# Linear attention: fine levels reduced to diagonal 32x32 blocks, with compact masked copies

## The chip, the cores and the metric

The kernel runs on one NeuronCore of a Trainium2 chip. The metric is the device time of one execution in microseconds, the median over several runs. A measurement of this kernel tells a change from no change at about 0.2%, which is about 4 us.

## The reference, cut to what matters

The program computes two transformer blocks over 512 tokens. The change lies in the gated linear attention of the first block: 4 heads, 64 key channels and 128 value channels each, run forward and backward, with a decay for each channel. Inside a chunk every pair of a query i and a key j has its own decay:

```python
rel = cum[:, :, :, None, :] - cum[:, :, None, :, :]
decay = jnp.exp(jnp.where(mask[:, :, None], rel, -jnp.inf))
attn = jnp.einsum('bhid,bhjd,bhijd->bhij', qc, kc, decay)
o = o_inter + jnp.einsum('bhij,bhje->bhie', attn, vc)
```

`o_inter` is the query, decayed, times the state that the earlier chunks left.

## The kernel before, in words

The kernel takes tiles of 128 tokens (4 of them, for 4 heads) and builds the 128 by 128 matrix of a tile and head, `attnT` (keys on partitions, queries in columns), level by level. `LEVELS` are the spans s = 64, 32, 16, 8, 4, 2, 1. At level s the pairs whose two tokens lie in neighbouring blocks of s inside one block of 2s are decayed through the boundary between the two blocks, so that the decay splits into a factor for the query and a factor for the key. Level 0 in the code (`li` = 0) is the diagonal, and `li` = 1 to 7 are the seven spans.

One level takes these steps, in this order:

- VectorE (`sums`, L1519 to L1532) writes four differences of running sums: two halves of `lk`, then two halves of `lq`, each of 128x512 elements.
- ScalarE (`level_decay`, L1410) takes the exponential of `lk`, then of `lq`, in place.
- GpSimd (`gla_gpsimd`, L1599) multiplies `lk` with the keys, and VectorE (L1549) multiplies `lq` with the queries.
- TensorE (`gla_level`, L1280) forms, for both heads of a pair, all tiles and both directions, the whole 128x128 products into four PSUM banks.
- The part of the level is copied out of PSUM into `attnT`: for `li` 1 and 2 by ScalarE in blocks (`blocks`, L1415), for `li` 0 and 3 to 7 by VectorE under a mask of 128 columns (`attention`, L1505), four instructions of 128x512 elements a level.

`lq` and `lk` have two buffers each (`lq_even`, `lq_odd`), so the steps of level `li` + 1 run while TensorE works on level `li`. VectorE does the copy of level `li` - 1 behind the sums of `li` + 1. GpSimd's and VectorE's programs are in a fixed order, written out by hand, and engines wait for each other by semaphores. A PSUM bank is taken by `claim`, which waits until the reader before has counted `bank_empty`.

Around this stage: level 0 is formed on TensorE (L1289) in the middle of four "spreads" (L1316, a transposition that spreads a norm factor over the columns, two heads ahead of level 0 and two behind it). Their results go through VectorE (L1246, L1239) and ScalarE (L1432) into `hh` and `hl`, which `mixed_values_chunk` (L1386) multiplies with a weight (L441). Its first chunk claims PSUM bank 1, which level 0 has used. After the last level TensorE adds the share of the states to the outputs (`from_states`, L1341), multiplies `attnT` with the values (`within`, L1347), sums squares (`output_sums`, L1357), and the output projection follows (L441).

On TensorE a float32 matmul is two records in the trace, so "x32" there stands for 16 matmuls of the program.

The constants of the first block lie in one tile, `csta`, which one transfer loads (L2892). Before, it holds eight masks of 128 columns.

## Time and profile before

| | |
|---|---|
| median of 3 runs | 2075.94 us (2074.49 to 2076.79) |
| the profiled execution | 2078.38 us, of which its span from the first to the last instruction is 2076.4 us |
| TensorE (PE) busy | 1976.8 us of the span, 9954 matmul records |
| VectorE (DVE) busy | 929.1 us |
| ScalarE (ACT) busy | 745.2 us |
| GpSimd (POOL) busy | 706.1 us |
| mean granted clock of TensorE | 0.969 of full speed |

Busy time is an average over stages with different limits. The stage that the change touches lies between about 341 and 443 us of the span; the rest of the program is untouched, save for the load of `csta` at 50 us. A profile's row tells its start, its length, the engine, the line of the kernel, what is written and read, how many equal ones are merged, and in brackets how long the engine sat idle before it and who ended that.

### The profile page before, as it was taken

The numbers are of one execution on the slowest core, as the hardware profiler recorded it, in microseconds if no ns is written. First come the engines' busy times: TensorE is split into PE (matmuls) and PEld (weight loads), VectorE is DVE, ScalarE is ACT, GpSimd is POOL, SyncE is SP. The second block draws the span as 40 slices with busy tenths as digits, with TensorE's granted clock in tenths as the row PEclk, the third lists the DMA queues.
The fourth block names the chain that finished last, engine by engine and source line by source line (L and its number), as shares of the span: only waits on it lengthen the run. The fifth ranks groups of instructions, "written<-read, shape, count | busy, mean of one in ns | idle before, by whom it ended". The sixth has DMA issues, their size and how long they took to land.

```text
span 2076.4 us, 25531 instructions
## 1 busy us (share of the span) xinstructions
PE 1976.8 (95%) x9954; PEld 1561.8 (75%) x9954; DVE 929.1 (45%) x1358; ACT 745.2 (36%) x1235; POOL 706.1 (34%) x296
## 2 busy tenths in 40 slices
PE   7999988799999999999999989889999999999998
PEld 5787857687888888788888867656876768888886
DVE  2642586844444420444443334676776522332102
ACT  4533364533322311432322134546255432323222
POOL 1421110423444444344444433220421343444442
PEclk9999998879999999999999999999999999999999
DMA  7751110013444442334445422200210222232231
GB/s 309 299 210 41 42 62 1 21 41 104 150 146 147 161 173 91 112 132 146 147 149 194 173 77 82 71 32 21 92 62 31 82 81 82 100 94 98 92 100 61
DMA packets 60125, 223.60 MB, mean 108 GB/s; under 512 B 6800, under 2 KB 7056, under 8 KB 58256
## 3 DMA queue, kind: packets, MB, share of 16 engines
q1 hardware_dynamic: 59472, 220.13, 30.7%
q10 hardware_dynamic: 576, 2.43, 0.3%
q8 instruction: 50, 0.82, 0.2%
q14 instruction: 27, 0.22, 0.0%
HBM read 220.43 MB, written 2.10 MB: 107 GB/s over the span
## 4 chain that ended last, share of the span: by engine, by line
PE 86%; DVE 7%; ACT 3%; issue 2%; DMA 1%; SPq 0%; POOL 0%; DVEq 0%; ACTq 0%
PE ps L441 75%; DVE neg_max L1197 1%; PE ps L587 1%; DMA mod_w<-mod_w 1%; PE ps L2231 1%; ACT w_hi L454 1%; PE ps L1052 1%; PE ps L2402 1%; PE ps L2423 0%; PE ps L1071 0%; PE ps L2253 0%; PE ps L974 0%; PE ps L2411 0%; DVE ps L693 0%; DMA raw<-stream 0%
## 5 line engine op out<-in xcount | busy, mean ns | idle before, releaser
L1820 POOL TENSOR_TENSOR w_lo<-raw,w_hi 128x1024 fp32r<-128x1024 f32 x276 | 668.1, 2421 | 1295.9 <-ACT w_hi L454 696.0
L441 PE MATMUL ps<-hh,w_hi 128*128 128x512 f32 (+1 forms) x1512 | 605.3, 400 | 21.2 <-DVE hl L679 8.8
L441 PE MATMUL ps<-hl,w_hi 128*128 128x512 f32 (+1 forms) x1512 | 595.9, 394 | 0.0
L441 PE MATMUL ps<-hh,w_lo 128*128 128x512 f32 (+1 forms) x1512 | 595.2, 394 | 0.0
L441 PEld LDWEIGHTS ps<-hh,w_hi 128*128 128x128 f32 (+1 forms) x1512 | 287.7, 190 | 94.7 <-issue 30.3
L441 PEld LDWEIGHTS ps<-hh,w_lo 128*128 128x128 f32 (+1 forms) x1512 | 287.5, 190 | 62.4
L441 PEld LDWEIGHTS ps<-hl,w_hi 128*128 128x128 f32 (+1 forms) x1512 | 288.0, 190 | 58.1
L1793 ACT ACTIVATE w_hi<-raw 128x1024 fp32r<-128x1024 f32 x126 | 133.8, 1062 | 478.0 <-PE ps L441 478.0
L507 DVE SCALAR_TENSOR_TENSOR mod_raw<-mod_raw,cond_ada 128x1024 f32<-128x1024 f32 x72 | 118.1, 1642 | 245.6 <-DMA mod_raw<-late 245.6
L441 PE MATMUL ps<-act_hi,w_hi 128*128 (+1 forms) x528 | 208.8, 396 | 0.0
L441 PE MATMUL ps<-act_lo,w_hi 128*128 (+1 forms) x528 | 208.8, 396 | 0.0
L441 PE MATMUL ps<-act_hi,w_lo 128*128 (+1 forms) x528 | 208.8, 396 | 0.0
L1853 DVE TENSOR_TENSOR act_lo<-prod,act_hi 128x512 fp32r<-128x512 f32 x66 | 157.6, 2388 | 57.5 <-ACT act_hi L1798 57.5
L1812 ACT ACTIVATE w_hi<-raw 128x1024 fp32r<-128x1024 f32 x60 | 63.6, 1061 | 266.2 <-PE ps L441 266.2
L454 ACT ACTIVATE w_hi<-raw 128x1024 fp32r<-128x1024 f32 x90 | 94.7, 1055 | 146.9 <-PE ps L441 144.5
L1850 DVE TENSOR_TENSOR prod<-silu,ps 128x512 f32<-128x512 f32 x66 | 45.4, 688 | 222.3 <-PE ps L441 208.9
L441 PEld LDWEIGHTS ps<-act_lo,w_hi 128*128 128x128 f32 x528 | 99.2, 188 | 24.0
L441 PEld LDWEIGHTS ps<-act_hi,w_lo 128*128 128x128 f32 x528 | 99.2, 188 | 24.0
L441 PEld LDWEIGHTS ps<-act_hi,w_hi 128*128 128x128 f32 x528 | 99.2, 188 | 23.9
L1677 DVE SCALAR_TENSOR_TENSOR xT<-ps,half_gate_f,xT 128x512 f32<-128x512 f32 x16 | 11.2, 749 | 137.7 <-PE ps L441 137.7
L1677 DVE SCALAR_TENSOR_TENSOR xT<-ps,mod,xT 128x512 f32<-128x512 f32 x24 | 17.5, 750 | 92.7 <-PE ps L441 92.6
L507 DVE SCALAR_TENSOR_TENSOR early_raw<-early_raw,cond 128x1024 f32<-128x1024 f32 x32 | 48.5, 1542 | 15.5 <-DMA early_raw<-early 9.5
(432 smaller groups left out, 2340.7 us busy)
## 6 DMA issues: line engine op xcount, KB each, us to landing
raw<-stream SPq DMA_DIRECT2D x284, 512.0 KB, 3.3
mod_raw<-late SPq DMA_DIRECT2D x72, 512.0 KB, 4.4
early_raw<-early SPq DMA_DIRECT2D x32, 512.0 KB, 6.4
mod_w<-mod_w SPq DMA_DIRECT2D x8, 1024.0 KB, 20.1
xT<-xT SPq DMA_DIRECT2D x2, 1024.0 KB, 6.3
xT<-xT ACTq DMA_DIRECT2D x2, 1024.0 KB, 6.3
out<-fin SPq DMA_DIRECT2D x8, 256.0 KB, 2.2
csta<-csta SPq DMA_DIRECT2D x1, 1344.0 KB, 5.7
```

The lines of the kernel that those rows point to most:

```text
L441: mm = pe.matmul(out, w, r, start=first and i == 0, stop=last and i == 2)
L454: act.activation(halves_of(g)[0][:, :], raw[slot_of[g] % RING][:, :], ACT.Copy).then_inc(S("w_hi_ready"), 1)
L507: dve.scalar_tensor_tensor(out=slot, in0=slot, scalar=1.0, in1=condition, op0=ALU.mult, op1=ALU.mult, accum_out=to)\
L587: mm = pe.matmul(ps[32 * q:32 * q + 32, ba, 0:tokens], c("one").broadcast_to([P, 32]), squares(key, k, tokens), start=(k < 4), stop=(k >= ...
L1052: mm = pe.matmul(flat[:, r * 1024 + a:r * 1024 + z], dq[rows, h, qt * P:(qt + 1) * P], dk[rows, h, a:z], start=True, stop=True)
L1197: dve.tensor_reduce(neg_max[u % 2][:, comp:comp + 1], flat[:, r * 1024:r * 1024 + NALL], AX, ALU.max, negate=True)\
L1677: dve.scalar_tensor_tensor(out=xT[:, m, :], in0=ps[:, b, :], scalar=gate(m), in1=xT[:, m, :], op0=ALU.mult, op1=ALU.add)\
L1793: act.activation(w_hi[g % SPLIT][:, :], raw[n % RING][:, :], ACT.Copy).then_inc(S("w_hi_ready"), 1)
L1812: act.activation(w_hi[g % SPLIT][:, :], raw[n % RING][:, :], ACT.Copy).then_inc(S("w_hi_ready"), 1)
L1820: pool.tensor_tensor(lo[:, :], raw[n % RING][:, :], hi[:, :].bitcast(F32), ALU.subtract)\
L1850: dve.tensor_tensor(prod[j][:, :], silu[j][:, :], ps[:, b + 1, :], ALU.mult).then_inc(bank_empty(b + 1), 1)
L1853: dve.tensor_tensor(act_lo[:, at], prod[j][:, :], act_hi[:, at].bitcast(F32), ALU.subtract).then_inc(S("act_ready"), 1)
```

## The change

- `li` 0 and 3 to 7 (the diagonal and the spans up to 16) form only the four diagonal blocks of 32x32 of each tile: 64 matmuls with 32 weight columns and 32 moving columns each, for 16 with 128 and 128. They write two PSUM banks, one for each head of a pair (`fine_bank`), 256 columns of each.
- VectorE's masked copy goes from those banks to a compact tile `diag` ([128, 4, 4, 32]), two instructions of 128x256 elements a level for four of 128x512. The masks have 32 columns.
- After the last level `diag` is put into the diagonal blocks of `attnT`: two copies on VectorE and two on ScalarE, 32 partitions and 512 elements each. `within` waits for all four (`diag_ready`).
- The last level (s = 1) has no `lk` of its own: its factor is 1, so TensorE reads the keys. Two of VectorE's sums, one of ScalarE's exponentials and one of GpSimd's products go away.
- The copies of `li` 1 and 2 on ScalarE no longer wait for the level before, since they write other blocks.
- `from_states(0)` moves from ahead of the last level to ahead of the last but one, and `from_states(1)` from behind the last level to ahead of it.
- `csta` shrinks from 2688 to 1856 columns.

```diff
-for _name, _w in (("rot", 128), ("cos", 512), ("sin", 512), ("carry", 512), ("levels", 128 * (1 + len(LEVELS)))):
+for _name, _w in (("rot", 128), ("cos", 512), ("sin", 512), ("carry", 512), ("fine", 32 * (1 + len(LEVELS) - COARSE))):
...
+    fine_bank = {0: 0, 3: 4, 4: 6, 5: 4, 6: 6, 7: 4}
+    def gla_level(pe, li):
...
+        if li in fine_bank:
+            for half in range(2):
+                claim(pe, fine_bank[li] + half, ("level", li, half))
+            for u in range(2 * NT):
+                for half in range(2):
+                    rows = slice(64 * half, 64 * half + 64)
+                    for o in range(0, P, 32):
+                        at = (u % 2) * N + (u // 2) * P + o
+                        mm = pe.matmul(ps[o:o + 32, fine_bank[li] + half, u * 32:u * 32 + 32], k[rows, at:at + 32], q[rows, at:at + 32],
+                                       start=True, stop=True)
+                    if u == 2 * NT - 1:
+                        mm.then_inc(bank_full(fine_bank[li] + half), 1)
+            return
...
         for li in range(1, len(LEVELS) + 1):
-            if li == len(LEVELS):
+            if li == len(LEVELS) - 1:
                 pe.wait_ge(S("qe_ready"), 2)
                 read(pe, ("u", len(directions) - 1, 4))
                 from_states(0)
+            if li == len(LEVELS):
+                from_states(1)
             pe.wait_ge(S("lq_ready"), li)
-            pe.wait_ge(S("lk_ready"), li)
+            if li < len(LEVELS):
+                pe.wait_ge(S("lk_ready"), li)
             gla_level(pe, li)
-        from_states(1)
-        for b in range(4):
-            read(pe, ("level", len(LEVELS), b))
+        pe.wait_ge(S("diag_ready"), 4)
         within(0)
...
+        for o in (0, 32):
+            act.activation(attnT[o:o + 32, :, :, o:o + 32], diag[o:o + 32, :, :, :], ACT.Copy).then_inc(S("diag_ready"), 1)
...
         def attention(li):
-            mask = ca("levels", li * P, (li + 1) * P).unsqueeze(1).unsqueeze(1).broadcast_to([P, 2, 2, P])
-            for b in range(4):
+            at = 32 * (li - COARSE if li else 0)
+            mask = ca("fine", at, at + 32).unsqueeze(1).unsqueeze(1).broadcast_to([P, NT, 2, 32])
+            for half in range(2):
...
-            mark("level_sums", dve.tensor_tensor(to_k[:, :, 0, :], mid_f, fw[:, :, 0, :], ALU.subtract))
-            mark("level_sums", dve.tensor_tensor(to_k[:, :, 1, :], mid_b, bw[:, :, 1, :], ALU.subtract))
+            if s > 1:
+                mark("level_sums", dve.tensor_tensor(to_k[:, :, 0, :], mid_f, fw[:, :, 0, :], ALU.subtract))
+                mark("level_sums", dve.tensor_tensor(to_k[:, :, 1, :], mid_b, bw[:, :, 1, :], ALU.subtract))
...
         attention(len(LEVELS))
+        for o in (64, 96):
+            dve.tensor_copy(attnT[o:o + 32, :, :, o:o + 32], diag[o:o + 32, :, :, :]).then_inc(S("diag_ready"), 1)
...
-        for li in range(1, len(LEVELS) + 1):
+        for li in range(1, len(LEVELS)):
             pool.wait_ge(S("lk_decay"), li)
             pool.tensor_tensor(lk[li % 2][:, :], lk[li % 2][:, :], k, ALU.mult).then_inc(S("lk_ready"), 1)
```

On TensorE, from level 5 (s = 4) to the products with the values, the program of before reads as follows (a matmul of the program is one here; L1289 is a level, L1341 the states' share, L1347 the product with the values):

```order
L1289 MATMUL ps<-lq_odd,lk_70 128x128 x16
L1289 MATMUL ps<-lq_even,lk_69 128x128 x16
L1341 MATMUL ps<-qe,states 128x128 x16
L1289 MATMUL ps<-lq_odd,lk_70 128x128 x16
L1341 MATMUL ps<-qe,states 128x128 x16
L1347 MATMUL ps<-attnT,vt 128x128 x12
```

and the changed one, where L1301 is a level, L1364 the states' share and L1370 the product with the values:

```order
L1301 MATMUL ps<-lq_odd,lk_70 32x32 x64
L1364 MATMUL ps<-qe,states 128x128 x16
L1301 MATMUL ps<-lq_even,lk_69 32x32 x64
L1364 MATMUL ps<-qe,states 128x128 x16
L1301 MATMUL ps<-lq_odd,gkx 32x32 x64
L1370 MATMUL ps<-attnT,vt 128x128 x12
```

Both shares of the states have moved one place up, and the last level now stands directly ahead of the products with the values.

On VectorE, from the product for level 6 (L1549) to the outputs (L1567), before:

```order
L1549 TENSOR_TENSOR lq_even<-lq_even,gqx 128x1024
L1529 TENSOR_TENSOR lk_70<-cumx 128x512
L1530 TENSOR_TENSOR lk_70<-cumx 128x512
L1531 TENSOR_TENSOR lq_odd<-cumx 128x512
L1532 TENSOR_TENSOR lq_odd<-cumx 128x512
L1516 COPY_PREDICATED attnT<-csta,ps 128x4x128 x4
L1549 TENSOR_TENSOR lq_odd<-lq_odd,gqx 128x1024
L1516 COPY_PREDICATED attnT<-csta,ps 128x4x128 x8
L1567 SCALAR_TENSOR_TENSOR og<-ps,vec,rT 128x512 x2
```

and of the change (L1583 is the product, L1549 the masked copy):

```order
L1583 TENSOR_TENSOR lq_even<-lq_even,gqx 128x1024
L1565 TENSOR_TENSOR lq_odd<-cumx 128x512
L1566 TENSOR_TENSOR lq_odd<-cumx 128x512
L1549 COPY_PREDICATED diag<-csta,ps 128x8x32 x2
L1583 TENSOR_TENSOR lq_odd<-lq_odd,gqx 128x1024
L1549 COPY_PREDICATED diag<-csta,ps 128x8x32 x4
L1600 COPY attnT<-diag 32x16x32 x2
L1605 SCALAR_TENSOR_TENSOR og<-ps,vec,rT 128x512 x2
```

The two sums for `lk` are gone, the masked copies are half as many and a quarter of the elements, and two copies into `attnT` stand behind the last one.

## Rows read from the trace of the kernel before

**Rows 1.** The page, part 1: busy time, share of the span, instructions of each engine.

```profile
PE 1976.8 (95%) x9954; PEld 1561.8 (75%) x9954; DVE 929.1 (45%) x1358; ACT 745.2 (36%) x1235; POOL 706.1 (34%) x296
```

**Rows 2.** The chain that ended last, around level 0: start us, us, what.

```profile
339.80 1.94 PE ps L1316 x8
341.74 4.89 PE ps L1289 x32
346.63 1.02 PE ps L1316 x8
347.65 4.72 issue
352.37 4.93 PE ps L441 x12
```

**Rows 3.** Timeline of VectorE between level 0 and the first chunk.

```profile
347.25 0.75 DVE L1246 SCALAR_TENSOR_TENSOR t<-od,gain_dn,ps 128x512 f32<-128x512 f32 x1 [4.12 <-PE ps L1316]
...
350.98 2.48 DVE L1514 TENSOR_TENSOR attnT<-ps,csta 128x512 f32<-128x512 f32 x4
```

**Rows 4.** Timeline of all engines but TensorE, levels 5 to 7.

```profile
408.32 1.22 DVE L1549 TENSOR_TENSOR lq_odd<-lq_odd,gqx 128x1024 f32<-128x1024 f32 x1
...
410.78 1.06 ACT L1413 ACTIVATE lk<-lk 128x1024 f32<-128x1024 f32 x1 [3.73 <-DVE lk L1530]
...
411.85 2.58 DVE L1516 COPY_PREDICATED attnT<-csta,ps 128x512 f32<-128x512 uint32 x4
411.92 2.37 POOL L1603 TENSOR_TENSOR lk<-lk,gkx 128x1024 f32<-128x1024 f32 x1 [3.62 <-ACT lk L1413]
411.98 1.06 ACT L1413 ACTIVATE lq_even<-lq_even 128x1024 f32<-128x1024 f32 x1
414.30 1.24 DVE L1549 TENSOR_TENSOR lq_even<-lq_even,gqx 128x1024 f32<-128x1024 f32 x1
...
420.29 1.24 DVE L1549 TENSOR_TENSOR lq_odd<-lq_odd,gqx 128x1024 f32<-128x1024 f32 x1
```

**Rows 5.** Timeline of TensorE: levels 2, 5 and 6, states' share, values.

```profile
388.81 2.82 PE L1289 MATMUL ps<-lq_even,lk 64*128 64x128 f32 x32 [0.48 <-DVE lq_even L1549]
...
409.59 3.79 PE L1289 MATMUL ps<-lq_odd,lk 64*128 64x128 f32 x32 [1.27 <-DVE lq_odd L1549]
415.59 5.13 PE L1289 MATMUL ps<-lq_even,lk 64*128 64x128 f32 x32 [2.21 <-DVE lq_even L1549]
422.92 3.79 PE L1341 MATMUL ps<-qe,states 64*128 64x128 f32 x32 [2.20 <-DVE attnT L1516]
...
431.73 2.94 PE L1347 MATMUL ps<-attnT,vt 128*128 128x128 f32 x24
```

**Rows 6.** Timelines of VectorE and GpSimd, level 3.

```profile
392.29 2.27 DVE L1549 TENSOR_TENSOR lq_odd<-lq_odd,gqx 128x1024 f32<-128x1024 f32 x1 [1.12 <-ACT lq_odd L1413]
...
391.13 2.35 POOL L1603 TENSOR_TENSOR lk<-lk,gkx 128x1024 f32<-128x1024 f32 x1 [4.44 <-ACT lk L1413]
```

**Rows 7.** Windows: stretch, length, busy by engine, granted clock (PEclk), DMA share, GB/s.

```profile
412.00:416.00 4.00, 1.79 (x11) 1.50 (x10) 4.00 (x6) 1.04 (x1) 2.28 (x1) 0.50 0.00 0
...
428.00:430.00 2.00, 2.00 (x32) 2.00 (x32) 1.52 (x3) 0.00 (x0) 0.00 (x0) 0.94 0.44 166
```

**Rows 8.** Timeline of TensorE: small or narrow matmuls elsewhere in the program.

```profile
1518.09 0.24 PE L2402 MATMUL ps<-step,table_part 128*32 128x128 bf16 x3
...
1518.39 0.22 PE L2402 MATMUL ps<-step,table_half 128*32 128x128 bf16 x1
...
357.23 1.31 PE L1329 MATMUL ps<-vt,kdT 128*64 128x128 f32 x20
```

**Rows 9.** Around the load of `csta`: the chain, a window, TensorE's wait.

```profile
51.42 8.58 DMA raw<-stream
...
60.00:70.00 10.00, 7.83 (x33) 4.52 (x32) 7.82 (x9) 8.01 (x15) 4.52 (x2) 0.83 1.01 399
...
65.01 0.92 PE L587 MATMUL ps<-sq_context,cst 128*32 128x256 f32 x4 [1.99 <-ACT sq_context L624]
```

More of the change, by code:

```diff
@@ L41 @@
 LEVELS = [64, 32, 16, 8, 4, 2, 1]
+COARSE = 2
 GRID_W = 64
@@ L232, in build @@
     lq = [sb("lq_even", [P, 2 * N]), lq_odd]
+    top[0] = region_dn
+    diag = sb("diag", [P, NT, HEADS, 32])
     top[0] = region
@@ L1418, in blocks @@
                 at_bank = full(act, ("level", li, b))
-                read(act, ("level", li - 1, b))
                 got = ps[:, at_bank, :].rearrange("p (t h i) -> p t h i", t=2, h=2)
@@ L1450, in gla_scalar @@
         split_slots(act, firsts["mix1"] + 1)
+        read(act, ("level", len(LEVELS), 0))
+        read(act, ("level", len(LEVELS), 1))
+        for o in (0, 32):
+            act.activation(attnT[o:o + 32, :, :, o:o + 32], diag[o:o + 32, :, :, :], ACT.Copy).then_inc(S("diag_ready"), 1)
         def output_high(h):
@@ L1522, in sums @@
             if li >= 3:
-                full(dve, ("level", li - 2, 3))
+                full(dve, level_done(li - 2))
             fw, bw = halves(cumx[:, 0, :], s), halves(cumx[:, 1, :], s)
@@ L1562, in gla_vector @@
         attention(len(LEVELS))
+        read(dve, ("level", len(LEVELS), 0))
+        read(dve, ("level", len(LEVELS), 1))
+        for o in (64, 96):
+            dve.tensor_copy(attnT[o:o + 32, :, :, o:o + 32], diag[o:o + 32, :, :, :]).then_inc(S("diag_ready"), 1)
         def gated_output(h):
@@ L2962, in constants @@
     put(first, CSTA, "carry", (t % P != 0)[None, :])
-    levels = [2.0 * np.eye(P)] + [(p[:, None] // (2 * s) == p // (2 * s)) & (p[:, None] // s != p // s) for s in LEVELS]
-    put(first, CSTA, "levels", np.concatenate(levels, axis=1))
+    here = p[:, None] % 32
+    there = np.arange(32)
+    fine = [2.0 * (here == there)] + [(here // (2 * s) == there // (2 * s)) & (here // s != there // s) for s in LEVELS[COARSE:]]
+    put(first, CSTA, "fine", np.concatenate(fine, axis=1))
     return stay, first
```

21 lines of the change are left out of this document (14 added, 7 removed).

## The prediction

> **What bounds the kernel now.** I read the page first. TensorE is busy for 95% of the span [rows 1], so what counts are the places where it waits or does little work for its time. Then I followed the chain of waits through the stage of the change, and read the timelines engine by engine, since the chain alone does not say who would be late next.
>
> Around level 0 the chain runs through TensorE itself. Two spreads are done, then the level's 32 records take 4.89 us, then come the other two spreads, and then TensorE stands still for 4.72 us until the first chunk of the projection [rows 2]. The timelines say what it stands for: the spread behind level 0 releases VectorE at 347.25, VectorE works through to 350.98, and there it copies level 0 out of four banks [rows 3]. The chunk claims bank 1, the second of the four. The copies start 0.6 us apart, so bank 1 is free near 352.3, and the chunk starts at 352.37. Level 0 and half of its copy are both on the path.
>
> From level 4 on the kernel runs in a cycle of 6.0 us: VectorE's product for `lq` starts at 408.32, 414.30 and 420.29 [rows 4]. Inside a cycle VectorE has no free time: product, four sums, four masked copies of 0.6 us. But a second chain has the same length. From the start of one product it is 2.46 us to ScalarE's exponential of `lk` (410.78), then GpSimd's product from 411.92 to 414.29. VectorE's next product starts at 414.30, right at its end. The exponential of `lq` ended at 413.04 and does not hold it. That GpSimd holds VectorE's product back is seen where no masked copy lies between: at level 3 the product is issued at 392.29 and takes 2.27 us instead of 1.2, ending 1.1 us after GpSimd's product that ran from 391.13 to 393.48 [rows 6]. The masked copies read PSUM and run beside GpSimd at their usual pace [rows 4].
>
> TensorE waits in this cycle. At the end it has the states' share (start 422.92, held by VectorE's copy of level 6 out of the banks that it claims), level 7, the second share, and the product with the values at 431.73 [rows 5].
>
> **A term at the front.** The transfer of one weight slot is on the chain for 8.58 us, until 60.0 [rows 9]. It is issued behind `csta`. Behind its landing comes ScalarE's chain, for which TensorE waits 1.99 us at 65.01 [rows 9]. `csta` loses 832 of 2688 columns, 128 x 832 x 4 bytes = 0.43 MB. At 399 GB/s, what the engines moved there [rows 9], that is 1.1 us. I take -1.0; it is -1.1 at most, and zero at least, if other transfers fill the place.
>
> **The cost of a small level (X).** A level of the new kind has 64 matmuls, 128 records with 32 moving columns. This is the unknown on which the sum hangs. From below: 24 bf16 records with 32 weight columns, six groups of four that go to four column strips, lie between 1518.09 and 1518.61 [rows 8]; first to last start is 0.3 us, 12.5 ns a record, with 128 moving columns each. 128 records at that pace are 1.6 us. From above: 20 float32 records with 64 weight columns take 1.31 us, some 55 ns from start to start [rows 8], which makes 7.0 us; the level itself has 88 ns a record at the high clock (2.82 us for 32) [rows 5], which makes 11.3 us. Those two move 128 columns in float32, four times what the new records move, and weights of two to four times the width. In form (narrow weights, neighbouring records in different strips) the first row is nearest. I take X = 2.0 us at the low clock and keep 1.6 to 4.
>
> The Trainium skill, in TensorE: Matmul & The Clock Gate, in its part on the gap of 56 ns, says that starts never come closer than about 25 ns however few columns are moved, and that firmware decoding costs about 62 ns a matmul in a long stream. By it X would be about 3.2 us, and 7.9 us with firmware decoding. The burst shows 12.5 ns, but is only 24 records long, so no row here refutes either for a stream of 128.
>
> **The sum.**
> 1. Level 0: 4.9 to 2.0 us, -2.9. The spreads behind it now fall where the clock is low: 8 spreads took 1.94 us ahead of the level and 1.02 behind it [rows 2]; VectorE needs the first four, so +0.4. The copy of bank 1 ends after 2 x 0.35 instead of 2 x 0.6 us: -0.6 (a copy of 256 elements costs between half of 0.61 and all of it; I take 0.35). Together -3.1.
> 2. Levels 1 to 3 and the cycles of levels 4 to 6: 0. VectorE saves 1.7 us of copies in each, but the cycle stays at 6.0 us because GpSimd's product sets it. TensorE's longer or shorter levels are covered by the wait ahead of each (1.27 and 2.21 us [rows 5]).
> 3. Level 7 has no `lk`. From the product at 414.30, two sums of 0.6 follow, and the exponential of `lq` starts at about the +2.46 where that of `lk` stood: 416.8, ends 417.8. GpSimd is idle, so the product for level 7 starts at 417.9 instead of 420.29.
> 4. TensorE's own order then decides. Level 5 from 409.6 to 411.6, the states' share 3.8 us [rows 5] to 415.4, level 6 at 415.6 to 417.6, the second share to 421.4, level 7 to 423.4. The old wait for the bank behind level 6 is gone.
> 5. Behind level 7 TensorE now waits: two masked copies (0.8 us), then two copies of 512 elements on VectorE, and beside them two on ScalarE, at 0.6 us each, with hops 0.4: 2.4 us. `within` starts at 425.8 instead of 431.73 [rows 5]: -5.9. What queues behind `diag_ready` is all of `within`, and ScalarE's squares.
> 6. The clock. It was granted in full (2.4 GHz) from 428 on, after TensorE had been busy without a break from 422.9, and at half (1.2 GHz) from 412 to 416, where it was busy for 1.79 of 4 us [rows 7]. The changed kernel has small matmuls, then a wait of 2.4 us, ahead of `within`, so I expect the low clock there. The spreads, also 128x128, show the price: 0.92 us for 8 [rows 2], 2.8 us for the 24 records of `within` that took 2.94. With a little of the sums behind them, +3.0. Bounds: 0, and +6 if the sums of squares run low too.
>
> Together -1.0 - 3.1 - 5.9 + 3.0 = -7.0 us. The profiled execution would go from a span of 2076.4 to 2069.4 and, with the 2.0 us that lie around it, from 2078.4 to 2071.4. The runs' median was 2.4 below that execution, so I predict 2069.0.
>
> X counts once in level 0 and three times at the end, so the sum is -7.0 + 4 (X - 2). Below 2.0 the last part gives less, since level 6 waits for `lq`.
>
> **The rivals.**
> - *The stream of records has a floor of its own.* If 128 records do not keep the pace of a burst of 24 and take twice its 12.5 ns each, X = 3.2 and the sum is -2.2 us, which a measurement can't tell from nothing. For it: no stream here is as dense for as long. Against: the burst goes to four strips as the new records do, and shows no such floor [rows 8]. Chance 0.23. This is the rival that the Trainium skill's rule above speaks for.
> - *TensorE becomes the bound.* Each record costs as in the narrow float32 row, 55 ns: X = 7.0. Level 0 then takes 2.1 us more than before, and each of the last three levels delays the values. The sum is +13 us, 2082. It decides from X = 3.75 on (29 ns a record), and a slowdown shows from X = 4.8 (37 ns). For it: 256 instructions a level where 64 were. Against: that row moves four times the columns with twice the weights. Chance 0.13.
> - *VectorE's relief shortens the cycles too.* If its product did not wait for GpSimd, it would start at 413.1 instead of 414.3, and TensorE's order would start 1.2 us sooner at level 5: -8.2. Against: the held product [rows 6]. Chance 0.06.
> - *The clock stays up.* Then step 6 is 0 and the sum -10. For it: from 409.6 on TensorE would hardly pause. [...] Chance 0.08.
> - The forecast itself, -7 with X between 1.6 and 2.7: 0.50.
>
> **Numbers.** 0.2% are 4.2 us. Forecast, clock and cycle rivals (0.64) nearly all lie beyond it; the forecast loses 0.04 to no change where the clock costs 6 us. So faster 0.60, no change 0.27, slower 0.13. The range reaches to the clock rival with X = 1.6 (about -11 to -12) and past the floor rival with the dearer clock (about +1): 2064 to 2076.5, leaving 0.2 outside, most of it on the slow side.
>
> **What would show it.** Level 0 in the trace: 128 records in about 2 us, and the first chunk some 3 us earlier against the spread ahead of it. VectorE's products of levels 5 and 6 still 6.0 us apart, the one of level 7 at 3.6 us behind. `within` some 2.4 us behind the last level, at the low clock (24 records in over 5 us). The slot at 60.0 landing 1 us sooner. I am wrong if the small levels take over 3.75 us, if the stage of squares behind `within` loses more to the clock than 3 us, or if `diag_ready` is late because VectorE's copies are held by something that I don't see.

## The result, and the profile after

The changed kernel took 2065.45 us (median of 4 runs, 2061.4 to 2066.24) against 2075.72 us for the kernel before, run beside it. The ratio is 0.9943 with a 95% interval of 0.9929 to 0.9956: faster, by some 10 to 12 us. The forecast was 2069.0, so the sign was right and the size too small. The profiled execution took 2066.24 us with a span of 2064.4, which is 12.0 less than the span before.

The page's busy row of the changed kernel, to be held against [rows 1]:

```profile
PE 1959.6 (95%) x10526; PEld 1542.8 (75%) x10530; DVE 921.6 (45%) x1346; ACT 745.1 (36%) x1236; POOL 702.8 (34%) x295
```

TensorE is still busy for 95% of the span; it has 572 more records and 17 us less busy time.

The chain that ended last, around level 0 (answers to [rows 2]):

```profile
340.31 1.06 PE ps L1339 x8
341.37 1.22 PE ps L1301 x80
342.59 1.02 PE ps L1339 x8
343.61 4.19 issue
347.80 2.54 PE ps L445 x6
```

Level 0 went from 4.89 us to 1.22 in the chain (1.29 in the timeline, for all 128 records). The spreads ahead of it took 1.06 instead of 1.94, because the clock was full here and half before.

VectorE, GpSimd and ScalarE, levels 5 to 7 and the copies into `attnT` (answers to [rows 4]):

```profile
402.18 2.27 DVE L1583 TENSOR_TENSOR lq_odd<-lq_odd,gqx 128x1024 f32<-128x1024 f32 x1 [0.43 <-ACT lq_odd L1441]
407.98 2.27 DVE L1583 TENSOR_TENSOR lq_even<-lq_even,gqx 128x1024 f32<-128x1024 f32 x1 [0.44 <-ACT lq_even L1441]
412.58 1.22 DVE L1583 TENSOR_TENSOR lq_odd<-lq_odd,gqx 128x1024 f32<-128x1024 f32 x1 [0.43 <-ACT lq_odd L1437]
417.75 2.74 DVE L1600 COPY attnT<-diag 32x512 f32<-32x512 f32 x2
...
406.82 2.35 POOL L1641 TENSOR_TENSOR lk<-lk,gkx 128x1024 f32<-128x1024 f32 x1 [3.45 <-ACT lk L1441]
415.09 4.66 POOL L1858 TENSOR_TENSOR w_lo<-raw,w_hi 128x1024 fp32r<-128x1024 f32 x2 [5.92 <-ACT w_hi L458]
...
417.74 1.28 ACT L1482 ACTIVATE attnT<-diag 32x512 f32<-32x512 f32 x2 [1.78 <-DVE diag L1549]
```

The products of levels 5 and 6 now last 2.27 us instead of 1.22: with shorter masked copies in front (0.77 us instead of 2.58), they are issued while GpSimd works; level 6's ends 1.08 us behind GpSimd's product (410.25 and 409.17). Level 7's, with no work on GpSimd, lasts 1.22. The two copies into `attnT` take 2.74 us on VectorE and 1.28 on ScalarE.

TensorE from level 5 to the next projection (answers to [rows 5]):

```profile
404.50 1.47 PE L1301 MATMUL ps<-lq_odd,lk 64*32 64x32 f32 x118 [2.93 <-DVE lq_odd L1583]
407.41 0.34 PE L1301 MATMUL ps<-lq_odd,lk 64*32 64x32 f32 x10 [1.44 <-issue]
407.69 3.78 PE L1364 MATMUL ps<-qe,states 64*128 64x128 f32 x32
411.40 1.55 PE L1301 MATMUL ps<-lq_even,lk 64*32 64x32 f32 x128
...
420.54 4.31 PE L1370 MATMUL ps<-attnT,vt 128*128 128x128 f32 x24 [3.83 <-DVE attnT L1600]
424.69 1.84 PE L1380 MATMUL ps<-cst,sq 128*128 128x2 f32 x16
...
432.13 0.47 PE L445 MATMUL ps<-hh,w_hi 128*128 128x512 f32 x1 [1.82 <-DVE hl L1622]
```

A small level takes 1.55 us at the low clock, 12 ns a record. Level 5 stands still for 1.44 us ("issue", nothing that it waits for) with 10 records left. The product with the values starts at 420.54 instead of 431.73, at the low clock, after a wait of 3.83 us.

The two traces side by side, by start in the span:

| place | before | after | moved | forecast |
|---|---|---|---|---|
| spreads ahead of level 0 | 339.80 | 340.31 | +0.5 | -1.0 |
| first chunk behind it | 352.37 | 347.80 | -4.6 | -4.1 |
| VectorE's product, level 5 | 408.32 | 402.18 | -6.1 | -4.1 |
| VectorE's product, level 7 | 420.29 | 412.58 | -7.7 | -6.5 |
| product with the values | 431.73 | 420.54 | -11.2 | -10.0 |
| first chunk of the next projection | 443.03 | 432.13 | -10.9 | -7.0 |
| end | 2076.4 | 2064.4 | -12.0 | -7.0 |

Up to the values the sum is 1.2 us short. Most of the miss, 3.8 us, lies behind them, where the forecast charged the clock: 2.7 us of it up to the first chunk, 1.1 us behind.

### The profile page after: what moved, and what is told of

The parts are those of the page before. It is cut to its first block, busy times and chain, and to the rows that moved or that the text cites. A ratio compares the mean times of both kernels' runs of the same rounds, so it can differ in the third digit from the quotient of the medians.

```text
span 2064.4 us, 26644 instructions
## 1 busy us (share of the span) xinstructions
PE 1959.6 (95%) x10526; PEld 1542.8 (75%) x10530; DVE 921.6 (45%) x1346; ACT 745.1 (36%) x1236; POOL 702.8 (34%) x295
## 4 chain that ended last, share of the span: by engine, by line
PE 86%; DVE 7%; ACT 3%; issue 2%; DMA 1%; SPq 0%; DVEq 0%; ACTq 0%
PE ps L445 75%; PE ps L1056 1%; DMA early_raw<-early 1%; DMA mod_w<-mod_w 1%; PE ps L591 1%; DVE neg_max L1201 1%; PE ps L1075 1%; PE ps L2269 1%; PE ps L2440 1%; PE ps L2461 0%; DVE ps L697 0%; PE ps L2291 0%; PE ps L2431 0%; PE ps L978 0%; PE ps L2449 0%
## 5 line engine op out<-in xcount | busy, mean ns | idle before, releaser
L1715 DVE SCALAR_TENSOR_TENSOR xT<-ps,half_gate_f,xT 128x512 f32<-128x512 f32 x16 | 11.2, 750 | 137.7 <-PE ps L445 137.7
```

Source lines behind the costliest of these rows:

```text
L1715: dve.scalar_tensor_tensor(out=xT[:, m, :], in0=ps[:, b, :], scalar=gate(m), in1=xT[:, m, :], op0=ALU.mult, op1=ALU.add)\
```

## The experiments

For each run the table has the median, the ratio to the kernel before on the same chip with its interval, and three distances in its trace: **A** from the first spread ahead of level 0 to the first chunk, **B** from that chunk to the product with the values, **C** from there to the first chunk of the next projection. Distances leave out when the stage began, but each is read from one execution, and the clock that this one had is in it.

| kernel | us | ratio (95%) | A | B | C |
|---|---|---|---|---|---|
| before | 2075.72 | 1 | 12.57 | 79.36 | 11.30 |
| changed | 2065.45 | 0.9943 (0.9929-0.9956) | 7.49 | 72.74 | 11.59 |
| a1 changed, again | 2066.39 | 0.9952 (0.9939-0.9966) | 9.08 | 72.69 | 11.59 |
| a2 wide table | 2066.96 | 0.9956 (0.9942-0.9969) | 9.08 | 72.66 | 11.63 |
| a3 late states | 2065.84 | 0.9950 (0.9936-0.9963) | 9.09 | 72.85 | 12.03 |
| a4 last `lk` | 2069.22 | 0.9962 (0.9950-0.9974) | 8.62 | 74.59 | 14.32 |
| b1 late splits | 2064.89 | 0.9939 (0.9926-0.9953) | 9.09 | 70.83 | 13.13 |
| b2 late fill | 2064.69 | 0.9938 (0.9925-0.9952) | 8.56 | 73.09 | 11.83 |
| b3 wide level 0 | 2072.68 | 0.9977 (0.9967-0.9987) | 14.04 | 72.88 | 11.71 |
| b4 level 0 four times | 2077.45 | 1.0004 (0.9995-1.0013) | 18.14 | 73.19 | 11.90 |
| c1 wide levels 3-7 | 2069.56 | 0.9968 (0.9955-0.9980) | 9.09 | 77.45 | 11.86 |
| c2 before, no last `lk` | 2073.77 | 0.9989 (0.9980-0.9998) | 9.55 | 77.97 | 12.02 |
| c3 both fills | 2065.06 | 0.9950 (0.9936-0.9963) | 8.40 | 72.50 | 11.65 |
| c4 late splits and fills | 2063.24 | 0.9932 (0.9919-0.9946) | 9.09 | 71.13 | 11.56 |
| d1 small, halves apart | 2066.93 | 0.9954 (0.9941-0.9968) | 9.40 | 72.79 | 14.32 |
| d2 wide level 0, in turns | 2069.03 | 0.9962 (0.9949-0.9976) | 9.15 | 72.26 | 14.32 |
| d3 before, in turns | 2074.52 | 0.9990 (0.9981-0.9999) | 8.78 | 78.43 | 11.91 |
| d4 level 0 twice | 2070.14 | 0.9968 (0.9956-0.9980) | 9.95 | 72.52 | 14.31 |

The intervals are some 2.7 us to each side, so the medians don't part kernels that differ by one or two. How far the distances do is seen in the two traces of the changed kernel: B and C agree within 0.05 us, A differs by 1.6.

### The front term and the end of the stage

**a1.** The changed kernel again, for the others to stand beside.

> The changed kernel once more, as the measure for the three others of this chip. Every theory: about 11 us less than before, in the same places as in its profile (5 us around level 0, 6 to 7 us up to the product with the values, none lost behind it).

It gave the same B and C as the first time. A is 9.08 instead of 7.49; this time the clock was low through level 0 and the spreads behind it (1.55 and 1.97 us instead of 1.29 and 1.09); the chunk started at 348.10 all the same (347.80 the first time), since the stage began 1.3 us sooner.

**a2.** `csta` as wide as before:

```diff
-("fine", 32 * (1 + len(LEVELS) - COARSE))):
+("fine", 32 * (1 + len(LEVELS) - COARSE)), ("pad", 832)):
```

> csta is padded to its old 2688 columns, nothing else. If the shorter transfer is worth what the prediction took for it, this kernel is 1.0 us slower than the changed one, and the difference is still there when level 0 begins. My theory now: the slot behind csta lands about 0.7 us later, but nothing of it reaches level 0, because the waits behind it (the stretches at the half clock among them) differ by as much; 0 to 0.3 us slower at the end.

The spreads ahead of level 0 start at 339.19, against 339.02 in a1, and the span is 2064.8 against 2064.6. The medians are 0.6 us apart. One pair can't settle it, though: up to level 0 the changed kernel and thirteen of the experiments are the same program, and their spreads start anywhere from 336.45 (a4) to 340.31 us (the first trace), 338.7 on average. The four traces with the long table (before, a2, c2, d3) have them at 339.19 to 340.30, 339.9 on average. That is 1.1 us for the short table, with a scatter of about 1.1 us from one execution to the next. So the 1.0 us of the prediction is neither refuted nor measured well.

**a3.** The states' share back at its old places:

```diff
-            if li == len(LEVELS) - 1:
+            if li == len(LEVELS):
                 ...
                 from_states(0)
-            if li == len(LEVELS):
-                from_states(1)
 ...
+        from_states(1)
         pe.wait_ge(S("diag_ready"), 4)
```

> The first half of the states' share goes back behind level 6 and the second behind level 7. My theory: TensorE has both halves (3.8 and 2.2 us) between its last levels and the values instead of in waits of the cycle; the second half, 2.2 us or 3.8 at the half clock, then fills the wait of 3.8 us for the copies into attnT, so it costs nothing there, and the first half delays level 7 by some 1 to 2 us: 1 to 2 us slower. Rival: the place of the shares is worth most of what the last part won, 4 us or more slower. Second rival: level 7 waits for VectorE anyway and nothing changes, within 0.5 us.

B is 0.2 longer and the median is the same within the noise: the second rival, nothing changes. Level 7 ends 1.5 us later than in a1 (418.1 against 416.55), but the second share fills the wait for the copies, and the copies themselves took less. TensorE's timeline in a3, and GpSimd's and VectorE's:

```profile
418.02 2.06 PE L1364 MATMUL ps<-qe,states 64*128 64x128 f32 x32
420.71 2.94 PE L1370 MATMUL ps<-attnT,vt 128*128 128x128 f32 x24 [0.64 <-DVE attnT L1599]
```

```profile
415.25 4.67 POOL L1857 TENSOR_TENSOR w_lo<-raw,w_hi 128x1024 fp32r<-128x1024 f32 x2 [5.92 <-ACT w_hi L458]
419.14 1.52 DVE L1599 COPY attnT<-diag 32x512 f32<-32x512 f32 x2
```

The copies are issued 0.8 us before GpSimd's `w_lo` ends at 419.92, and take 1.52 us instead of 2.74. The product with the values then ran at the full clock (2.94 us), but a low stretch came behind it, and C is 0.4 us longer than in a1. So in this kernel the place of the shares was worth nothing at the end.

**a4.** Level 7 keeps its `lk`: the conditions on the last level are taken out on all four engines.

```diff
-        k = lk[li % 2] if 0 < li < len(LEVELS) else gkx
+        k = lk[li % 2] if 0 < li else gkx
...
-            if s > 1:
-                mark("level_sums", dve.tensor_tensor(to_k[:, :, 0, :], ...
+            mark("level_sums", dve.tensor_tensor(to_k[:, :, 0, :], ...
...
-        for li in range(1, len(LEVELS)):
+        for li in range(1, len(LEVELS) + 1):
             pool.wait_ge(S("lk_decay"), li)
```

> Level 7 keeps its lk: two more sums on VectorE, one exponential on ScalarE, the product on GpSimd. The product of level 7 on VectorE then starts 5.8 us behind that of level 6 instead of 4.6 (the sums 1.2 later, and the product held by GpSimd's for another 1 us). My theory: the product ends 2.3 us later, level 7 ends 2.0 to 2.3 us later, and the whole is 2 to 2.5 us slower than the changed kernel. Rival: the sums are not on TensorE's path, since it still has the second states' share to do, and it is under 0.7 us slower.

The product of level 7 starts 5.81 us behind that of level 6 (411.70 and 405.89) instead of 4.60, and B is 1.9 longer, just short of the theory's 2.0 to 2.3. Its median is 2.8 us above a1's, more than the theory's 2 to 2.5; in the traced execution C was 2.7 us longer as well (below), and the stage began 2.6 us sooner.

**c2.** The same part alone, in the kernel before: level 7 without `lk`.

```diff
+        k = lk[li % 2] if 0 < li < len(LEVELS) else gkx[:, :, :].rearrange("p c n -> p (c n)")
...
+            if s > 1:
                 mark("level_sums", dve.tensor_tensor(to_k[:, :, 0, :], ...
...
-        for li in range(1, len(LEVELS) + 1):
+        for li in range(1, len(LEVELS)):
             pool.wait_ge(S("lk_decay"), li)
```

> The kernel before with one part of the change alone: level 7 takes gkx as it is, without the two sums, the exponential and GpSimd's product. My theory: alone it gains little, because TensorE has level 6 until 420.7, then waits for the copies of level 6 and has the states' share, level 7 and the second share in front of it; the product for level 7 is ready 2.4 us sooner, but the copies of level 6 behind it end where level 6 ends, so 0.5 to 1.3 us faster than before. Rival: the product of level 7 is what the end hangs on: 2.0 us or more faster, as taking it back cost the changed kernel about 2 us.

B is 79.36 - 77.97 = 1.4 us shorter, a little above the theory's span and below the rival's. The ratio, 2.3 us with an interval from 0.4 to 4.2, fits either.

**c1.** Wide levels 3 to 7 in two banks:

```diff
+            if li:
+                for half in range(2):
+                    for u in range(2 * NT):
+                        ...
+                        mm = pe.matmul(ps[:, fine_bank[li] + half, (u % 4) * P:(u % 4) * P + P], k[rows, at:at + P], q[rows, at:at + P], ...)
```

> Levels 3 to 7 are formed with 16 matmuls of 128 moving columns each, two banks as in the changed kernel; level 0 stays small (output leaves out right levels 3 to 7). My theory: the small levels are what shortens TensorE's end, levels 5 to 7 count in full. A wide level took 6.5 us in the run with a wide level 0, at the low clock; 3.8 to 5.1 us in the kernel before. With 4 to 6.5 us instead of 1.5 for three levels the product with the values comes 7 to 14 us later. Rival: VectorE's cycle of 5.8 us still sets the pace and only level 7 counts: 2.5 to 5 us later.

B is 4.8 us longer: less than the theory's 7 to 14. The number lies in the rival's range, but its mechanism is not what the trace has: from 399.57, the start of level 4, to the end of level 7 at 422.7 TensorE never waits, so VectorE's cycle does not set the pace. Levels 3 to 5 took 6.1 to 6.5 us each at the low clock. TensorE had been busy without a break since 399.57 when the clock rose at about 415; level 7, at the full clock, took 3.4.

### The copies into attnT

**b1.** ScalarE's splits of the next weights (and so GpSimd's `w_lo`) behind the copies:

```diff
-        split_slots(act, firsts["mix1"] + 1)
         ... the two copies into attnT ...
+        act.wait_ge(S("diag_ready"), 4)
+        split_slots(act, firsts["mix1"] + 1)
```

> ScalarE splits the ring's next weights only when the copies into attnT are done, so GpSimd's two w_lo (4.66 us) no longer lie beside VectorE's two copies. My theory: GpSimd holds VectorE's copies between two tensors in SBUF (2.74 to 3.13 us for two in the changed kernel, 1.52 where w_lo had ended first, in the run with late states). So the copies take 1.5 us, the product with the values starts 1.2 to 1.6 us sooner behind level 7, and the whole is 1.2 to 1.6 us faster than the changed kernel if the delayed weights are still in time. Rival: the copies are slow because they write 32 partitions with gaps; then they stay at 2.7 us or more and nothing is won. Second rival: the squares or the next chunk wait for ScalarE and GpSimd instead, and it is slower.

Its timeline, and a window of it:

```profile
417.50 0.87 DVE L1601 COPY attnT<-diag 32x512 f32<-32x512 f32 x2
418.83 4.30 PE L1370 MATMUL ps<-attnT,vt 128*128 128x128 f32 x24 [2.36 <-ACT attnT L1480]
419.94 4.67 POOL L1859 TENSOR_TENSOR w_lo<-raw,w_hi 128x1024 fp32r<-128x1024 f32 x2 [10.38 <-ACT w_hi L458]
...
427.00:437.00 10.00, 8.53 (x33) 7.37 (x33) 4.43 (x8) 1.94 (x4) 0.00 (x0) 0.50 0.06 20
```

The copies take 0.87 us instead of 2.74 to 3.13, and ScalarE's are last now. The edit moves ScalarE's splits as well as GpSimd's `w_lo`, but in the changed kernel the splits had ended at 415.96, before the copies began; only `w_lo` ran beside them. It is one copy that is held, until GpSimd's product has ended. The two copies in the changed kernel and in b1 (shortest, median and longest of the two in ns), and the splits in the changed kernel:

```profile
L1600 DVE COPY attnT<-diag x2: 423/1352/2282, 417.7 to 420.1; 32x512 f32<-32x512 f32 x2
L1601 DVE COPY attnT<-diag x2: 418/420/423, 417.5 to 418.0; 32x512 f32<-32x512 f32 x2
413.97 1.99 ACT L458 ACTIVATE w_hi<-raw 128x1024 fp32r<-128x1024 f32 x2
```

The held copy ended at about 420.03, 0.28 us behind the end of `w_lo` (419.75); in a3 it lasted 1.07 us and ended 0.28 us behind as well. That GpSimd held them is shown. B is 1.9 us shorter, more than expected. But C is 1.5 us longer: the clock was low for the whole of 427 to 437, where it had been full in the changed kernel (1.00 in its windows up to 448). What is left at the next chunk is 0.3 us.

### The clock

The granted clock of the changed kernel around the product with the values (windows; columns as in [rows 7]):

```profile
416.00:420.00 4.00, 0.70 (x77) 0.59 (x66) 3.13 (x3) 1.26 (x2) 3.75 (x2) 1.00 0.36 120
420.00:424.00 4.00, 3.46 (x18) 3.46 (x19) 1.10 (x3) 0.61 (x2) 0.00 (x0) 0.57 0.45 149
424.00:434.00 10.00, 8.18 (x66) 7.54 (x65) 5.25 (x10) 3.32 (x7) 0.00 (x0) 1.00 0.01 2
```

TensorE did little from 416 to 420, and behind that the clock is at half (1.2 GHz) for most of four microseconds, then full again.

**b2.** Work in TensorE's wait behind level 7:

```diff
+        read(pe, ("level", 6, 1))
+        for _ in range(2):
+            pe.matmul(ps[:, 7, 0:512], ident, gqx[:, 0, :], start=True, stop=True)
         pe.wait_ge(S("diag_ready"), 4)
```

> Adds two matmuls of 512 columns into a free bank in TensorE's wait for the copies into attnT; nothing else is changed. My theory: the wait of 3.8 to 4.2 us is why the clock is low in the first part of the product with the values, which takes 4.3 us instead of 2.9. With the wait filled it takes 2.9 to 3.0 and the whole is 1 to 1.4 us faster than the changed kernel. Rival: the clock falls because of the stages before, whatever TensorE does here; no change. Second rival: the low stretch only moves behind, into the sums of squares and spreads, as it did with late states; no change or up to 1 us slower.

TensorE's timeline in b2:

```profile
416.84 1.98 PE L1396 MATMUL ps<-gqx,cst 128*128 128x512 f32 x4
420.95 4.54 PE L1370 MATMUL ps<-attnT,vt 128*128 128x128 f32 x24 [2.13 <-DVE attnT L1603]
```

Half of the wait was filled and 2.13 us of it stayed; the product with the values still took 4.54. No gain clear of the noise, so the theory failed in this form: with half of the wait filled the clock was low all the same.

**c3.** The same, and fills ahead of levels 4 and 5:

```diff
+            if li in (4, 5):
+                pe.wait_ge(*bank_freed[fine_bank[li]])
+                for _ in range({4: 4, 5: 1}[li]):
+                    pe.matmul(ps[:, fine_bank[li], 0:512], ident, gqx[:, 0, :], start=True, stop=True)
```

> The fill in the wait behind level 7, and also four matmuls of 512 columns ahead of level 4 and one ahead of level 5, in waits. My theory: with more work in the waits of levels 4 and 5 the clock stays up through the product with the values (2.9 instead of 4.3 us), and some or all of it is given back by a low stretch later on, as in the run with the late fill alone (431 to 438): 0 to 1.5 us faster than the changed kernel. Rival: the low stretches do not depend on these waits at all and stand where they stood, from 390 to 414 and at 421; no change.

The mean granted clock of the run rose from 0.971 to 0.976, but B and C are those of the changed kernel within 0.2 us: the product with the values took 4.37 us after a wait of 3.20. The time is the same within the noise.

**c4.** The edits of b1 and c3, and one fill ahead of the next projection:

```diff
+        if key == "mix1":
+            pe.matmul(ps[:, bank0, 0:512], ident, gqx[:, 0, :], start=True, stop=True)
         for k in range(4):
             pe.wait_ge(S("og_ready"), k + 1)
```

> The late splits, the fills ahead of levels 4 and 5 and behind level 7, and one more ahead of the first chunk of the next projection. My theory: the product with the values starts 2 us sooner than in the changed kernel, as with late splits alone, and the low stretch from 427 to 437 that took 1.6 us of it back is gone: 2 to 3 us faster than the changed kernel. Rival: a low stretch comes anyway wherever the stage of squares lies, and it is 0.3 to 0.6 us faster, as late splits alone.

TensorE's timeline in c4:

```profile
417.63 1.98 PE L1400 MATMUL ps<-gqx,cst 128*128 128x512 f32 x4
420.06 2.94 PE L1370 MATMUL ps<-attnT,vt 128*128 128x128 f32 x24 [0.45 <-ACT attnT L1487]
```

With a wait of 0.45 us the product with the values runs at the full clock. The low stretch comes later, and C stays at 11.56. B + C is 82.69 us, 1.6 less than in a1, and the time is the lowest of all, 2063.24. The theory had 2 to 3 us and no low stretch in C, the rival 0.3 to 0.6; the trace lies between them, and of c4's five executions the traced one was the slowest (2065.88). Its interval overlaps those of b1, b2 and the changed kernel; that it beats the changed kernel is likely but not measured.

So the waits ahead of the product with the values go with its clock: after 0.45 and 0.64 us (c4, a3) it took 2.94 us, after 2.1 to 4.9 us 4.3 to 5.5. With no wait at all, in the kernel before, in c2 and in d3, it took 2.9.

**What the clock can cost** shows in runs that were made for something else. The windows of a1, then of d4, which are the same program from level 1 on:

```profile
424.00:427.00 3.00, 3.00 (x29) 3.00 (x29) 1.09 (x2) 0.78 (x3) 0.00 (x0) 1.00 0.00 0
430.00:436.00 6.00, 4.18 (x26) 3.31 (x23) 4.11 (x8) 2.18 (x5) 0.00 (x0) 1.00 0.01 3
```

```profile
424.00:427.00 3.00, 3.00 (x17) 3.00 (x15) 1.50 (x2) 0.60 (x2) 0.00 (x0) 0.50 0.00 1
430.00:436.00 6.00, 4.53 (x25) 4.16 (x25) 3.67 (x6) 1.91 (x4) 0.00 (x0) 0.58 0.01 3
```

In d4 the values start after the same wait (4.22 us; 4.23 in a1), the clock stays low for longer and falls again behind them. C is 14.31 instead of 11.59. The same C stands in a4, d1 and d2. The kernel before has 11.30, with a low stretch of its own: clock 0.54 in the window from 438 to 444. Against the kernel before, C is 0.3 to 3.0 us longer, mostly near one end or the other (b1, with 1.8, lies between). No edit here chooses between them, and each kernel but the changed one was traced once, so a second reading stands untested: that the same kernel has a short C in one execution and a long one in another. For it: d1's traced execution took 2070.83 us and another of its five 2070.46, the other three 2064.93 to 2066.93, with the mean clock at 0.969 and at 0.971 to 0.974. Against: d4's six all took 2068.75 or more, a1's five 2068.82 or less.

### What a level costs

**b3.** Level 0 alone wide again, one half of the rows after the other:

```diff
+            if li == 0:
+                for half in range(2):
+                    for u in range(2 * NT):
+                        ... as in c1
```

> Only level 0 is formed again with 64x128 weights and 128 moving columns, 16 matmuls into the same two banks and with the same masked copies (the copies then take numbers that are not the diagonal blocks: the output leaves out a right level 0). My theory: level 0 is on the path with all of its time, 32 records take 2.8 us at the high clock and 4.9 at the low one instead of 1.3 to 1.55, and the whole is 1.5 to 3.3 us slower than the changed kernel, the first chunk by as much. Rival: half of the 5.1 us that the stage lost came from the smaller copies out of two banks; then the chunk moves by less than 1.5 us.

Level 0 in TensorE's timeline of this run:

```profile
341.69 6.51 PE L1301 MATMUL ps<-gqx,gkx 64*128 64x128 f32 x32
```

A is 14.04 instead of 9.08. The level grew by 6.51 - 1.55 = 4.96 us and A by 4.96: level 0 is on the path with all of its time, which is the theory. But 6.51 is above the 4.9 that the theory gave, and the chunk's 4.96 us above its 1.5 to 3.3.

**d2.** The same with matmuls that take turns between the row halves:

```diff
-                for half in range(2):
-                    for u in range(2 * NT):
+                for u in range(2 * NT):
+                    for half in range(2):
```

> Level 0 wide as in the earlier run, but the matmuls take turns between the row halves (the output leaves out a right level 0). My theory: matmuls on different halves of the rows overlap, so level 0 takes 3.8 us at the low clock or 2.1 at the high one, as the states' share of the same form and turns does, instead of 6.5; the first chunk is 0.8 to 2.3 us later than in the changed kernel, and not 5. Rival: the 6.5 us came from something else (writes to the same place twice, the banks); then it stays near 6.5.

Level 0 in TensorE's timeline of this run:

```profile
338.80 2.08 PE L1301 MATMUL ps<-gqx,gkx 64*128 64x128 f32 x32
```

This was at the full clock, 65 ns a record. The states' share, with turns too, took 2.06 us for 32 records at the full clock and 3.78 at the low one. The order of the halves is the reason for the 6.51, as the theory says. The first chunk did not come 0.8 to 2.3 us later: A is nearly that of a1, since level 0 and the spreads behind it ran at the full clock here and at the low one in a1.

**d3.** Turns in all levels of the kernel before:

```diff
-            for j in range(4):
-                ...
+            for j in range(4):
+                for half in range(2):
+                    at_bank = b + half + 4 * (li % 2)
```

> The kernel before with one edit: in all levels the matmuls take turns between the row halves, in pairs of banks; same result. My theory: level 0 goes from 4.89 to 3.8 us (low clock) or from 2.8 to 2.1 (high), and TensorE's end (levels 6 and 7) gets 1 to 2 us shorter, but VectorE's cycle of 6.0 us stays: 1 to 2.5 us faster than before. Rival: level 0 and the end are bound by VectorE's copies out of the banks, and the second bank comes free later with turns: no change.

Level 0 in TensorE's timeline, in c2 (the old order) and in d3, both at the full clock:

```profile
341.13 2.82 PE L1290 MATMUL ps<-gqx,gkx 64*128 64x128 f32 x32
341.29 2.06 PE L1291 MATMUL ps<-gqx,gkx 64*128 64x128 f32 x32
```

A is 0.77 us shorter than in c2, as much as the level, and B is 0.9 us shorter than in the kernel before. The ratio, 2.1 us faster (0.2 to 3.9), lies inside the theory's range.

**d1.** The small levels without turns:

```diff
-            for u in range(2 * NT):
-                for half in range(2):
+            for half in range(2):
+                for u in range(2 * NT):
                     for o in range(0, P, 32):
```

> All small levels issue the 32 matmuls of the lower row half first and then those of the upper, same result. If the turns between halves are what makes records cheap, a small level goes from 1.3 to 1.55 us to 2.5 us or more, as a wide one goes from 118 ns a record in turns (states' share, low clock) to 203 in groups of eight matmuls; the whole is 1 to 3 us slower. If the four column strips are (my theory), it stays at 12 to 13 ns a record and nothing changes.

Level 0 in TensorE's timeline of this run:

```profile
341.43 1.87 PE L1301 MATMUL ps<-gqx,gkx 64*32 64x32 f32 x128
```

1.87 us instead of 1.55 at the low clock, 14.6 ns a record: above the theory's 13, far below the 2.5 us of the other reading. The turns between the halves give 0.3 us. Whether the rest of the small form's pace comes from the column strips or from moving 32 columns instead of 128, no run tells apart.

**b4, d4.** Level 0's stream issued four times, and twice:

```diff
+            for again in range(4 if li == 0 else 1):
                 for u in range(2 * NT):
```

> The 64 small matmuls of level 0 are issued four times over, 512 records in one stream, with the same result. My theory: 12 ns a record at either clock, also in a long stream, so the stream takes 6.1 us instead of 1.3 to 1.55 and the whole is 4.6 to 4.8 us slower than the changed kernel. Rival: the pace of 128 records comes from instructions that were fetched ahead while TensorE waited; a longer stream falls to 25 ns a record or worse, which makes 9.6 us more or above.

TensorE's timeline around level 0, and a window:

```profile
340.64 1.70 PE L1302 MATMUL ps<-gqx,gkx 64*32 64x32 f32 x138
342.61 1.54 PE L1302 MATMUL ps<-gqx,gkx 64*32 64x32 f32 x128 [0.26 <-issue]
346.33 1.54 PE L1302 MATMUL ps<-gqx,gkx 64*32 64x32 f32 x128 [2.19 <-issue]
349.79 1.46 PE L1302 MATMUL ps<-gqx,gkx 64*32 64x32 f32 x118 [1.92 <-issue]
...
343.00:351.00 8.00, 3.90 (x351) 3.62 (x340) 0.00 (x0) 0.00 (x0) 0.00 (x0) 0.50 0.02 6
```

> Level 0's small matmuls issued twice, 256 records. In the run with four times as many, 138 records ran at 12 ns, the next 128 ended 1.9 us behind them and each 128 after that took 3.5 to 3.7 us. My theory: the first 64 to 70 matmuls are those that lay ready while TensorE waited and worked on the spreads, so the second 64 cost 1.8 to 3 us instead of 1.5, and the whole is 2 to 3 us slower than the changed kernel. Rival: the slow pace sets in only for streams above 256 records, and it is 1.5 us slower.

TensorE's timeline of d4:

```profile
340.70 2.88 PE L1302 MATMUL ps<-gqx,gkx 64*32 64x32 f32 x256
```

The stream of 256 records ran at 11 ns each without a gap; my theory for d4 is wrong and its rival right. In b4, behind some 266 records, the long stream gets one new group of 128 in 3.72 us (342.61 to 346.33) and the next in 3.46, 27 to 29 ns a record or 54 to 58 ns a matmul, with nothing to wait for. That is the slower pace of b4's rival: A grew by 9.06 us, not by 4.7. Where the rival saw the cause, in instructions fetched ahead, is not shown. The median of d4 is 3.8 us above a1's; in the traces A is 0.9 us longer and C 2.7, the clock again.

## Why the prediction was too small

**The front term (-1.0)** did not show in the first trace, where the stage began 0.5 us later than before, nor clearly in one pair (a2). Over all traces the short table goes with a start 1.1 us sooner, beside a scatter as large (see a2), and `csta` lands 4.5 to 5.2 us after its issue instead of 5.4 to 5.8. So the term stays open, and the first trace's +0.5 hid it.

**Step 1 (-3.1)** was right in kind. b3 shows that level 0 counts in full. X was 1.29 us at the full clock and 1.55 at the low one, not 2.0. A fell by 5.1 us between the first two profiles and by 3.5 to a1, where the clock is low around level 0 as it was before; that is the comparison for this step, and it gives -3.5. At the full clock A was 9.55 in c2, which has the old level 0, so the step is worth 2.1 there. At the chunk the front term and step 1 together came out at -4.6 against -4.1.

**Step 2 (0)** is the first step that failed. Between the chunk and the product of level 5 the changed kernel won 6.1 - 4.6 = 1.5 us, 1.2 of it in the cycle of level 4. The timeline of VectorE in the kernel before, around level 4, and level 4's product in the changed kernel:

```profile
400.75 2.80 DVE L1549 TENSOR_TENSOR lq_even<-lq_even,gqx 128x1024 f32<-128x1024 f32 x1 [0.48 <-ACT lq_even L1413]
405.88 2.56 DVE L1516 COPY_PREDICATED attnT<-csta,ps 128x512 f32<-128x512 uint32 x4
...
395.85 2.80 DVE L1583 TENSOR_TENSOR lq_even<-lq_even,gqx 128x1024 f32<-128x1024 f32 x1 [0.48 <-ACT lq_even L1441]
```

The product of level 4 is held (2.80 us) in both kernels. Behind it VectorE had four sums and four masked copies before, and needed 7.57 us (400.75 to 408.32); now it needs 6.33 (395.85 to 402.18). The prediction read the cycle at levels 5 and 6, where both chains are equally long, and carried it over to level 4, where VectorE's was the longer. The rival of VectorE's relief, given 0.06, was right in this one cycle. In the next it won 0.2, and the held products of 2.27 us show GpSimd's grip, as forecast.

**Steps 3 to 5 (-5.9)** gave 4.9: from the product of level 6 to that of level 7 it is 4.60 us, where step 3 had 3.6, because level 6's product is itself held for 1.05 us. From there to the values it is 7.96 us, forecast 7.9. Two errors cancel inside it: level 7 ended 4.1 us behind the start of its product and not 5.5 (the X of 2.0, and the second share at the full clock), but the copies cost a wait of 3.83 us and not 2.4, since GpSimd held VectorE's (b1).

**Step 6 (+3.0)** is the step that failed most, by 3.8 us: behind the start of the product with the values the changed kernel lost 0.3 us up to the next chunk and won 1.1 behind it. It was right that the product with the values meets the low clock: 4.31 us instead of 2.94, after a wait. It was wrong to add this to a kernel before that was taken to have none. [rows 7] show its clock full at 428 to 430, but its own low stretch came behind, at 438 to 444 (0.54). The trace of the kernel before had it, and the sum left it out (its window; the columns are those of [rows 7]):

```profile
438.00:444.00 6.00, 4.53 (x21) 3.99 (x22) 3.54 (x7) 1.42 (x3) 0.00 (x0) 0.54 0.00 0
```

In the changed kernel the same work runs at the full clock (its window of 424 to 434 has 1.00). One low stretch changed places with another: C went from 11.30 to 11.59. Past the next chunk the changed kernel won another 1.1 us; before, the first matmuls of that projection still ran at the half clock (0.63 us each at 444.02, 0.40 at 432.68 now). A price of 3.0 us exists, in the traces of a4, d1, d2 and d4, but not in the changed kernel's two. What decides between the two stays open.

TensorE as the bound (X = 7) did not come either. The clock rival, -10, was nearest to the result, but by luck: it said that the clock stays up, and the clock fell.

## What to carry to other kernels

Before charging a stage with a low clock, read the granted clock of the same work in the kernel before, window by window up to the next long busy stretch, and charge only the difference, for a low stretch may only change places. Read a cycle that two chains bind equally at every turn, since in one of them either chain may be the longer. Let float32 matmuls on 64 rows take turns between the halves: level 0 of the kernel before took 2.06 us instead of 2.82 for it. Expect a long stream of small matmuls to slow down (b4, behind 133), and short ones to stand still now and then. Look at several executions before pricing a term of 1 us at the front of a long program, for here the start of the stage scattered by 3.9 us.

## What the runs showed of the hardware

- Matmuls on the two halves of the rows overlap. 32 records of 64x128 took, at the low clock, 3.78 us with turns at every matmul (states' share), 4.89 to 5.13 in groups of four matmuls (kernel before), and 6.51 in groups of eight (b3); at the full clock 2.06 (d3), 2.82 (c2), and 3.4 (c1, level 7). The Trainium skill (TensorEngine Tiling (Array Packing), in Tiling Modes) says that tiles load weights and multiply independently, which agrees.
- Small records (32 weight columns, 32 moving columns, float32) came every 12 ns at the low clock (1.55 us for 128) and every 10 ns at the full one (1.29 us).
- A copy on VectorE from SBUF to SBUF of 32 partitions took 0.42 us alone (b1). Issued beside a product on GpSimd, one of the two lasted 1.07 us (a3), 2.28 (changed kernel) and 2.46 (a1), and ended 0.3 us behind GpSimd's product. The Trainium skill (SBUF — State Buffer, in Who interferes with whom) counts such copies among those that can take the pair of ports shared with GpSimd; the trace agrees.
